# Hybrid block: the first down projection by seven products of quarter blocks per pair of outputs

## The reference

```python
def conv_ffn(h, w_up, conv_w, w_down):
    up = causal_dwconv(h @ w_up, conv_w)
    gate, val = jnp.split(up, [D_FF], axis=-1)
    return (jax.nn.silu(gate) * val) @ w_down
...
        h = rmsnorm(x, norm_ffn_g[l])
        x = x + conv_ffn(h, w_up[l], ffn_conv_w[l], w_down[l])
```

## Time and profile before

| | |
|---|---|
| runs | 1265.39 us median of 3 (1264.82 to 1266.54) |
| profiled execution | 1264.99 us, span 1263.3 us |
| PE, PEld busy | 1248.4 us (99%), 1003.6 us (79%) |
| DVE, ACT, POOL busy | 832.2 us (66%), 581.1 us (46%), 223.5 us (18%) |
| DMA | 130.01 MB, mean 103 GB/s |
| chain that ended last | PE 95%, of it line 842 82% |

### The profile page before, as it was taken

The page is one execution under the profiler, slowest core; times in us unless marked ns, Lnnn a source line. Parts: engine busy times, 40 slices in busy tenths (PEclk is TensorE's granted clock), DMA queues, the critical chain, the costliest instruction groups (busy, mean ns, idle before and its releaser), DMA issues.

```text
span 1263.3 us, 20146 instructions
## 1 busy us (share of the span) xinstructions
PE 1248.4 (99%) x6625; PEld 1003.6 (79%) x6625; DVE 832.2 (66%) x1709; ACT 581.1 (46%) x1053; POOL 223.5 (18%) x476
## 2 busy tenths in 40 slices
PE   8999999999999999999999999999999999999998
PEld 6777878878788788888888888888888776777776
DVE  6978777787777843444477773367764687794743
ACT  6655545445455432223344442244444465666632
POOL 2613304033040300001300000000004124440021
PEclk9999999999999999999999999999999999999999
DMA  6345263452634533333233323333224344333221
GB/s 191 76 118 142 73 152 91 117 132 78 156 89 119 131 102 85 99 100 100 84 102 99 100 75 100 113 95 100 81 84 109 102 117 118 84 87 97 81 71 67
DMA packets 283492, 130.01 MB, mean 103 GB/s; under 512 B 77296, under 2 KB 276271, under 8 KB 283445
## 3 DMA queue, kind: packets, MB, share of 16 engines
q1 hardware_dynamic: 283445, 129.42, 37.7%
HBM read 119.34 MB, written 10.06 MB: 102 GB/s over the span
## 4 chain that ended last, share of the span: by engine, by line
PE 95%; DVE 2%; ACT 1%; issue 1%; DMA 1%; SPq 0%; POOLq 0%; DVEq 0%; POOL 0%; ACTq 0%
PE gb L842 82%; PE gb L1290 2%; PE gd L1290 1%; PE gd L1240 1%; PE gd L1230 1%; PE gd L1218 1%; PE gd L935 1%; PE gd L943 1%; PE gd L1013 1%; PE gd L1024 1%; DMA raw<-in_w_in_dram 1%; DVE wlo L1843 0%; PE gd L1002 0%; ACT whi L1340 0%; PE gd L1001 0%
## 5 line engine op out<-in xcount | busy, mean ns | idle before, releaser
L842 PE MATMUL gb<-act_a,whi 128*128 128x512 f32 x2656 | 888.7, 398 | 0.3 <-DVE wlo L1843 0.2
L842 PEld LDWEIGHTS gb<-act_a,whi 128*128 128x128 f32 x2656 | 498.9, 188 | 111.9 <-issue 9.9
L842 PE MATMUL gb<-act_a,wlo 128*128 128x512 f32 x1408 | 548.9, 390 | 0.0
L1843 DVE TENSOR_TENSOR wlo<-raw,whi 128x1024 fp32r<-128x1024 f32 (+1 forms) x197 | 235.6, 1196 | 136.6 <-ACT whi L1340 134.7
L1340 ACT ACTIVATE whi<-raw 128x1024 fp32r<-128x1024 f32 (+1 forms) x210 | 215.7, 1027 | 217.4 <-PE gb L842 191.4
L842 PEld LDWEIGHTS gb<-act_a,wlo 128*128 128x128 f32 x1408 | 265.1, 188 | 48.4 <-issue 0.5
L842 PE MATMUL gb<-act_b,whi 128*128 128x512 f32 x432 | 152.9, 393 | 0.9 <-DVE wlo L1843 0.9
L842 PEld LDWEIGHTS gb<-act_b,whi 128*128 128x128 f32 x432 | 81.1, 188 | 18.8 <-DVE wlo L1843 1.4
L2745 POOL TENSOR_TENSOR zs<-zs,ca 128x512 f32<-128x512 f32 x3 | 4.2, 1397 | 321.3 <-ACT ca L1343 321.3
L842 PE MATMUL gb<-act_b,wlo 128*128 128x512 f32 x128 | 49.9, 390 | 0.0
L2700 POOL TENSOR_TENSOR Ue<-Ue,elt 128x60 f32<-128x60 f32 (+14 forms) x120 | 45.0, 375 | 9.4
(11 more groups left out here) (494 smaller groups left out, 1497.2 us busy)
## 6 DMA issues: line engine op xcount, KB each, us to landing
raw<-in_w_in_dram SPq DMA_DIRECT2D x102, 512.0 KB, 3.7
raw<-in_w_up_dram SPq DMA_DIRECT2D x44, 512.0 KB, 3.7
raw<-in_w_down_dram SPq DMA_DIRECT2D x16, 384.0 KB, 3.1
raw<-in_w_down_dram SPq DMA_DIRECT2D x16, 320.0 KB, 3.0
raw<-in_w_a_out_dram SPq DMA_DIRECT2D x8, 512.0 KB, 4.0
raw<-in_w_b_out_dram SPq DMA_DIRECT2D x8, 512.0 KB, 3.6
raw<-in_w_o_dram SPq DMA_DIRECT2D x8, 512.0 KB, 3.5
raw<-in_w_out_dram SPq DMA_DIRECT2D x8, 512.0 KB, 3.6
```

The costliest lines, as they stand in the source:

```text
L842: ins = pe.matmul(gb[:, b, :], l, r, start=(first and m == 0), stop=(last and m == len(todo) - 1))
L1843: dve.tensor_tensor(wlo[:, i % 2, 0:k * P], raw[:, i % 4, 0:k * P], whi[:, i % 2, 0:k * P].bitcast(F32), ALU.subtract).then_inc(split_read ...
```

## The change

For f = 0 alone, the two outputs of a pair, the even and odd inner blocks, and the two halves of the tokens form a product of 2 by 2 by 2 blocks. The change makes it with seven block products in place of eight, at the price of sums of weights (`weight_sum`, 128x768 each, four per pair), sums of activations (`token_sum`, 256 columns each, four per turn), and sums of results, of which some are made in PSUM by letting P6, P7 and P3 add into banks of P1 and P5. Each block product is a unit of 18 TensorE products of 256 columns in place of 512.

- TensorE (`seven`): 4 pairs of 7 units of 18 products, 504 products of 256 columns.
- SP: four loads per pair into the four `raw` slots. From the second pair on, they wait until the sums of the pair before are made (`weights_added`). Before, each load waited for one split.
- ScalarE (`down_high`, `token_high`): 28 high parts of 768 columns in place of 16, and high parts of the token sums.
- VectorE: 28 low parts (`down_low`), 28 additions to `xT` (`down_out`; six of 256 columns per pair and one of 512), 14 of the 16 weight sums (`add_weights`, 128x768), and in the last turn three low parts of token sums (`token_low`).
- GpSimd: four token sums per up turn, their low parts for all but the last turn, and the first pair's first two weight sums.
- The f = 0 up turns are written out on ScalarE and VectorE where they were loops. High and low parts of even blocks are made for 256 tokens in place of 512.
- Semaphores get second uses and new names (`xT_ready` is `copied`, `hn_ready` is `scaled_or_added`, `zeros_ready` is `pool_tiles`).

```diff
+SEVEN = 7
+FIRST_PAIR = ("P1", "P5", "P2", "P4", "P6", "P3", "P7")
+OTHER_PAIR = ("P1", "P2", "P4", "P5", "P6", "P3", "P7")
+WEIGHTS_OF = {"P1": 0, "P2": 1, "P4": 3}
+SUM_OF = {"P5": 0, "P6": 1, "P3": 2, "P7": 3}
+SUM_AT = (1024, 1792, 2560, 0)
+BLOCKS = FF_CUT[0] // 2
+HALF = T // 2
...
+        def token_half(name, i, low):
+
+            first, second = slice(0, HALF), slice(HALF, T)
+            even, odd = (slot((FF_LO if low else FF_HI) + 2 * i + q) for q in range(2))
+            both, last = spare[3 * i + low], spare[3 * i + 2]
+            return {"P1": even[:, first], "P5": even[:, second], "P2": odd[:, first], "P3": odd[:, second],
+                    "P6": both[:, first], "P7": both[:, second], "P4": last[:, second if low else first]}[name]
+
...
+        def weight_sum(m):
+
+            return sums[:, SUM_AT[m]:SUM_AT[m] + BLOCKS * P]
...
-        N_UP[1] = N_DN[0] + 2 * KD
+        N_UP[1] = N_DN[0] + SEVEN * KD // 2
...
+        def weight_sums_done(p, m):
+
+            return 4 * p + ((1, 2, 3, 4) if p == 0 else (1, 3, 4, 2))[m]
...
+                if f == 0:
+                    even_odd = w_dn_v[:, 0:FF_CUT[0], :].rearrange("p (k s) n -> p k s n", s=2)
+                    for p in range(KD // 2):
+                        for m in (0, 2, 3, 1) if p else range(4):
+                            q, s = DOWN[m]
+                            if p == 0:
+                                sp.wait_ge(split_ready, N_DN[0] + m - 3)
+                            else:
+                                sp.wait_ge(weights_added, 4 * p - (1 if p > 1 and m != 1 else 0))
+                                used = [w for w, k in WEIGHTS_OF.items() if k == m]
+                                if used:
+                                    sp.wait_ge(split_ready, N_DN[0] + SEVEN * (p - 1) + pair_order(p - 1).index(used[0]) + 1)
+                            dst = raw[:, raw_at(p, m), 0:kh * P].rearrange("p (k n) -> p k n", k=kh)
+                            at = (2 * p + q) * P
+                            sp.dma_start(dst, even_odd[:, :, s, at:at + P]).then_inc(raw_landed[raw_at(p, m)], 16)
+                    sp.wait_ge(weights_added, 2 * KD)
+                    continue
+                for m, (q, s) in enumerate(DOWN_CROSSED):
...
+            def seven(p):
+
+                order = pair_order(p)
+                banks = ({"P1": gd[:, 0, :], "P2": gd[:, 1, :], "P4": gd[:, 2, :], "P5": gd[:, 3, :]} if p % 2 == 0 else
+                         {"P1": gb[:, 3, :], "P2": gb[:, 0, :], "P4": gb[:, 1, :], "P5": gb[:, 2, :]})
+                into = {"P6": "P1", "P7": "P1", "P3": "P5"}
+                read_first = {"P6": "P1", "P7": "P6", "P3": "P5"}
+                for at, name in enumerate(order):
+                    n = N_DN[0] + SEVEN * p + at
+                    pe.wait_ge(hi_ready, n + 1)
+                    if name in read_first:
+                        pe.wait_ge(out_read, R_DN[0] + SEVEN * p + order.index(read_first[name]) + 1)
+                    bank = banks[into.get(name, name)][:, 0:HALF]
+                    for j in range(BLOCKS):
+                        last = p == 0 and j == BLOCKS - 1
+                        if last and name in ("P1", "P2"):
+                            pe.wait_ge(up_hi, 2 * j + (1 if name == "P1" else 2))
+                        elif last and name in ("P5", "P6", "P4"):
+                            pe.wait_ge(copied, KD + 3 * j + 1 + ("P5", "P6", "P4").index(name))
+                        hi = whi[:, n % 2, j * P:j * P + P]
+                        pe.matmul(bank, hi, token_half(name, j, 0), start=(j == 0 and name not in into), stop=False,
+                                  skip_group_check=True)
+                        if last:
+                            continue
+                        if p == 0 and name in ("P1", "P2"):
+                            pe.wait_ge(up_lo, 2 * j + (1 if name == "P1" else 2))
+                        elif p == 0 and name == "P5":
+                            pe.wait_ge(pool_tiles, 1 + 3 * j + 1)
+                        elif p == 0 and name in ("P6", "P4"):
+                            pe.wait_ge(pool_tiles, 1 + 3 * j + (2 if name == "P6" else 3))
+                        pe.matmul(bank, hi, token_half(name, j, 1), start=False, stop=False, skip_group_check=True)
+                    pe.wait_ge(split_ready, n + 1)
+                    for j in range(BLOCKS):
+                        ins = pe.matmul(bank, wlo[:, n % 2, j * P:j * P + P], token_half(name, j, 0), start=False,
+                                        stop=(p > 0 and j == BLOCKS - 1), skip_group_check=True)
+                    if p == 0:
+                        j = BLOCKS - 1
+                        if name in ("P1", "P2"):
+                            pe.wait_ge(up_lo, 2 * j + (1 if name == "P1" else 2))
+                        elif name in ("P5", "P6", "P4"):
+                            pe.wait_ge(pool_tiles, 2 + 3 * j + ("P5", "P6", "P4").index(name))
+                        ins = pe.matmul(bank, whi[:, n % 2, j * P:j * P + P], token_half(name, j, 1), start=False, stop=True,
+                                        skip_group_check=True)
+                    ins.then_inc(unit_done, 1)
...
+            def down_high(n):
+
+                p, name = down_set(n)
+                if name in WEIGHTS_OF:
+                    m = WEIGHTS_OF[name]
+                    sc.wait_ge(raw_landed[raw_at(p, m)], raw_count(p, m))
+                    src = raw[:, raw_at(p, m), 0:BLOCKS * P]
+                else:
+                    m = SUM_OF[name]
+                    sc.wait_ge(weights_added, weight_sums_done(p, m))
+                    src = weight_sum(m)
+                sc.wait_ge(unit_done, n - 1)
+                sc.activation(whi[:, n % 2, 0:BLOCKS * P], src, ACT.Copy).then_inc(hi_ready, 1)
...
+            def down_low(n):
+
+                p, name = down_set(n)
+                src = raw[:, raw_at(p, WEIGHTS_OF[name]), 0:BLOCKS * P] if name in WEIGHTS_OF else weight_sum(SUM_OF[name])
+                dve.wait_ge(hi_ready, n + 1)
+                dve.tensor_tensor(wlo[:, n % 2, 0:BLOCKS * P], src, whi[:, n % 2, 0:BLOCKS * P].bitcast(F32),
+                                  ALU.subtract).then_inc(split_ready, 1)
...
+            def add_weights(m, p):
+
+                w = lambda k: raw[:, raw_at(p, k), 0:BLOCKS * P]
+                for k in ((2, 3), (0,), (1,), ())[m]:
+                    dve.wait_ge(raw_landed[raw_at(p, k)], raw_count(p, k))
+                if p:
+                    name = [s for s, k in SUM_OF.items() if k == m][0]
+                    dve.wait_ge(split_ready, N_DN[0] + SEVEN * (p - 1) + pair_order(p - 1).index(name) + 1)
+                elif m == 2:
+                    dve.wait_ge(out_read, R_DN[0])
+                elif m == 3:
+                    dve.wait_ge(pool_tiles, 1 + 3 * BLOCKS)
+                if m in (1, 2):
+                    dve.wait_ge(weights_added, weight_sums_done(p, m - 1))
+                a, b, op = ((w(2), w(3), ALU.add), (weight_sum(0), w(0), ALU.subtract), (w(1), weight_sum(1), ALU.subtract),
+                            (w(0), w(2), ALU.subtract))[m]
+                dve.tensor_tensor(weight_sum(m), a, b, op).then_inc(weights_added, 1)
+
...
+            def down_sums(n):
+
+                p, at = divmod(n - N_DN[0], SEVEN)
+                for m in ({2: (2, 3)} if p == 0 else {0: (3, 1), 1: (2,)}).get(at, ()):
+                    add_weights(m, p)
+                if at == SEVEN - 1 and p < KD // 2 - 1:
+                    add_weights(0, p + 1)
...
+            down_next(N_DN[0] + 3)
+            token_low("P6")
+            token_low("P4")
+            down_out(N_DN[0])
+            down_out(N_DN[0] + 1)
+            for n in range(N_DN[0] + 2, N_UP[1]):
+                down_out(n)
+                down_next(n + 2)
+                down_sums(n)
...
+            def token_sum(m, i):
+
+                g, t = gated(i), token_sums(i)
+                first, second = slice(0, HALF), slice(HALF, T)
+                dst, a, b = ((t[:, 0:HALF], g[:, second], g[:, first]), (t[:, T:T + HALF], vc[:, second], g[:, second]),
+                             (t[:, HALF:T], vc[:, second], t[:, 0:HALF]), (t[:, HALF + T:2 * T], vc[:, first], t[:, HALF:T]))[m]
+                pool.wait_ge(up_ready, 2 * i + (2 if m else 1))
+                if m >= 2:
+                    pool.wait_ge(scaled_or_added, KD + 4 * i + m)
+                pool.tensor_tensor(dst, a, b, ALU.subtract).then_inc(scaled_or_added, 1)
...
+            for i in range(BLOCKS):
+                if i:
+                    token_low("P6", i - 1)
+                    token_low("P4", i - 1)
+                token_sum(0, i)
+                if i < BLOCKS - 1:
+                    token_low("P5", i)
+                else:
+                    add_weights(0)
+                    add_weights(1)
+                for m in range(1, 4):
+                    token_sum(m, i)
```

(64 more changed lines are left out.)

151 lines of the change are left out of this document (131 added, 20 removed).

## The result

The changed kernel takes **1269.0 us** (median of 9 runs, 1268.0 to 1269.8) beside 1265.4 for the kernel before (9 runs): a ratio of 1.0028, 95% interval 1.0020 to 1.0037, so 3.6 us slower, where 2.7 less were forecast. The profiled execution took 1268.99 us, 4.0 more than that of before.

What follows compares the result with a forecast made beforehand. TensorE was taken to bound the kernel (busy 99%): 58.0 us of products plus waits of 0.5, 1.0, 2.0, 0.6 and 0.6 make a stage of 62.7 in place of 65.3 us, so 1262.7 us, range 1260 to 1267.

Steps and rivals of the forecast that it cites:

- TensorE's products: First down projection: 504 products of 256 columns at 115 ns take 58.0 us, a gain of 7.3 us before waits.
- the prediction's own upper case: First down projection with products at 120 ns and waits of 3.7 us: stage 64.2 us.
- What costs nothing: Up turns: added ScalarE work, GpSimd's 5.6 us of sums per turn and written-out loops cost no time.
- GpSimd and VectorE block each other: Rival, last up turn: token parts come 2 to 3 us late, stage 65.2, kernel 1265.3 us; chance 0.05.
- the rule: Skill's rule, doubted by the prediction: two-SBUF-input VectorE instructions contend with GpSimd ones reading SBUF; the loser waits a whole instruction.
- The five waits: TensorE waits in the first and second pair and behind the stage: 0.5, 1.0, 2.0, 0.6 and 0.6 us.
- wait 3: Before P2 of the second pair: its weights, loaded last behind the first pair's sums, come late; 2.0 us.
- wait 4: Before P5 of the second pair: its low part comes late in VectorE's list; 0.6 us.
- waits 1 to 3: Before P6 and P3 of the first pair and P2 of the second: 0.5, 1.0 and 2.0 us.
- VectorE the bound: Rival, the stage's pairs: extra cost per VectorE instruction makes its list the limit, kernel 1270 us; chance 0.17.
- Writing out, up turns, ScalarE: Up turns: written-out loops are free, and ScalarE gains some 1.5 us per turn but stays under 21.8 us.
- Products that don't shrink: Rival, first down projection: 256 column products take 215 ns, stage 108 us, kernel 1308 us; chance 0.04.

Runs made afterwards that it cites:

- e4: The kernel before, with each first down projection product of 512 columns issued as two of 256; 1269.16 us.
- e7: The kernel before, with each first down projection product issued as two, of 384 and 128 columns; 1282.24 us.
- e1: The changed kernel, with the first pair's first two weight sums made by VectorE in place of GpSimd; 1268.15 us.
- e3: The changed kernel with the edits of both e1 and e2; 1264.74 us.
- e5: The kernel of e3, with the last turn's three token sums moved from GpSimd to VectorE and VectorE's list reordered as TensorE needs the parts; 1262.89 us.
- e6: The kernel of e3, with three GpSimd subtractions that nobody waits for where its two weight sums stood; 1266.29 us.
- e2: The changed kernel, with the second and fourth pair's weights loaded into idle space so the second pair's loads don't wait for the first pair's sums; 1266.11 us.

## Why the prediction was wrong

The forecast was a stage of 62.7 us and 1262.7; it came out as 68.45 and 1269.0, beyond the range's end at 1267. The 5.75 us that separate the two stages have two main parts.

**TensorE's products** (58.0 us forecast, 60.5 measured; 2.5 us). The mechanism was right and the size off. The 512 column row of this form allows 113.4 ns or, if the extra falls on each product alike, 120.0; the prediction took 115, "near the proportional end", because the fp32 rows of 512 and 128 columns are nearly in proportion. That step failed: fp32 products are another form, and e4 shows 120 for this one. By e7 a product of 128 columns costs about as much here as in fp32, so the two forms do not scale alike. With 120 and its waits of 3.7 us, the prediction's own upper case (64.2) would have stood as the forecast: 1.1 us below before, no change that the runs can tell. (The sum for 109 ns is 54.9 + 6.5 = 61.4 us, not 61.6; nothing hangs on it.)

**"What costs nothing"** (3.2 us). GpSimd's work was costed at nothing, and the weight sums "ready before 0". They were ready (751.81, against the stage's start at 751.86), and their values delayed nobody. But while they ran, VectorE lost 1.0 us on a low part and 1.5 on two convolution steps, and from 758.9 to 762.6 another 1.6 us beside the token sums. ScalarE's SiLU and its high part for P5 stand behind that convolution. VectorE's chain, forecast to end at 7.65 us after the stage's start, ended at 11.1 (its last low part of a token sum, 256 wide, ended at 762.98). The waits for P5, P2 and P4 came of it, 3.17 us, of which the forecast had none. The weight sums made those for P5 and P2 (1.94 us): with these sums on VectorE, 0.36 is left (e1, e3). The token sums made that for P4 (1.23 us), which stays in e1 and e3 and falls to 0.57 in e5; there GpSimd was late itself, with 256 wide sums of 1.0 to 1.4 us where 0.7 was estimated. The prediction had named P4's wait as what comes if GpSimd is late in the last turn, and gave it no time.

The rival "GpSimd and VectorE block each other" named this mechanism, with a chance of 0.05, and let it delay token parts only; its price was 2.5 us above the forecast stage.
```profile
1039.00 0.42 DVE L2482 MAX8 small<-selb 128x8 f32<-128x256 f32 x1
1039.53 0.41 DVE L2483 MATCH_REPLACE8 selb<-small,selb 128x256 f32<-128x256 f32 x1
```

Other rows of the kernel before did speak for the rule. GpSimd's sums of line 2728 took 1.86 us, all six of them beside a VectorE step with two SBUF inputs (line 2343), where operations of the same size took 1.27 to 1.30 us with VectorE idle (line 2773). Two of each:

```profile
L2728 POOL TENSOR_TENSOR zs<-zs,ca 128x512 f32<-128x512 f32 x2 | 3.7, 1856 | 130.7 <-ACT ca L1343 130.7
```
```profile
L2773 POOL TENSOR_TENSOR vc<-gate,vc x2: 1268/1282/1297, 1156.6 to 1207.8; 128x512 f32<-128x512 f32 x2
```

After the change, e6 agrees with the rule (0.77 to 1.49 us per convolution step), and so does line 2612, which has one input in PSUM and is not held. That the loser waits for a whole instruction, which the section says outright only of VectorE's two-port modes, is partly borne out: e6's low part lost 0.25 us, the steps 0.7 each, with GpSimd's instructions at 1.46.

**The five waits** were right in place, and their sum is 4.65 us against 4.7. That is in part luck: wait 3 is 0.57 longer than forecast and wait 4 0.35 shorter, and waits 1 to 3 kept their sizes as VectorE's list and TensorE ran late by about as much. P6's low part was made at t = 13.4 (from the stage's start) in place of 9.9, and TensorE wanted it at 13.1 in place of 9.55. The sums were made at t = 15.1 in place of 11.6, the last load landed at 23.5 in place of 19.0, and TensorE was ready for it at 22.0 in place of 18.0. For waits 3 and 4 e2 shows the cause, loads behind sums.

**VectorE the bound** didn't happen: third and fourth pairs run at TensorE's pace without a wait, with VectorE busy 13.2 of 15.8 us. **Writing out, up turns, ScalarE**: nothing lost, as said; the turn stays at 21.76 us with GpSimd's 7.7 us in it, where 5.6 were forecast, since VectorE holds GpSimd there too (low parts of 256 columns take 1.79 us in some places and 0.74 in others). **Products that don't shrink**: no, at 256 columns.

The chances: 0.16 for slower was too little. A forecast at the edge of what the runs can tell, on a middle value between 109 and 120 ns that no row of this form supported, should not have had 0.51 for faster.

## What to carry to other kernels

Work moved to an idle GpSimd can cost VectorE time wherever VectorE runs instructions with two SBUF inputs: compare durations of single instructions, not busy shares, and look for a stretch where VectorE works from PSUM or idles, or where the critical engine has slack. Price a smaller product from the same form's own row, with its fixed part kept whole, and don't carry that below the columns that were measured: 256 columns cost 120 ns, 128 about 113. Seven products in place of eight were worth 4.8 us here (65.3 less 60.5), so little that one chain of loads behind sums ate 3 of them. Before counting such a gain, lay out who must be early at the border of the stage; with spare buffers, these sums on VectorE and its list reordered, the same algorithm did win, by 0.19% (e5).

## What the runs showed of the hardware

A wait can cost more than its length. In e1, TensorE stood still for 2.5 us before P2 of the second pair. Busy time by stretch in e1 (columns as in the earlier trace rows, the granted clock third from the end):

```profile
770.00:772.00 2.00, 1.60 (x14) 1.40 (x12) 0.72 (x2) 0.00 (x0) 0.00 (x0) 1.00 0.66 193
772.00:774.00 2.00, 0.05 (x1) 0.05 (x1) 0.07 (x1) 0.94 (x2) 0.00 (x0) 0.89 0.02 7
774.00:775.00 1.00, 1.00 (x5) 1.00 (x6) 1.00 (x2) 0.64 (x1) 0.00 (x0) 0.50 0.00 0
...
776.00:777.00 1.00, 1.00 (x7) 1.00 (x6) 1.00 (x3) 0.00 (x0) 0.00 (x0) 0.51 0.00 0
777.00:778.00 1.00, 1.00 (x10) 1.00 (x10) 1.00 (x2) 0.21 (x1) 0.00 (x0) 1.00 0.00 0
```

Behind it the clock is 0.50, which is 1.2 GHz, for 3 us; the products are 213 ns apart, and 1.4 us are lost on top of the wait. The profiled execution of the change waited 2.5 us in the same place with the clock at 1.00:

```profile
774.00:776.00 2.00, 0.00 (x0) 0.00 (x0) 0.00 (x0) 0.60 (x1) 0.00 (x0) 1.00 0.04 11
```

So the same wait may or may not be followed by it. The mean clock of whole executions agrees: it is 0.997 or 0.998 in 8 of 11 of e1 and in 3 of 9 of the change (these three took 1269.4 to 1269.8 us), and 0.999 or more in all 43 of e2, e3, e5 and e6, which have no such wait.

Most waits inside TensorE's stream also cost some 0.1 us beyond themselves: the distance after one is 222 ns in place of 120 (24.44 to 24.66 us after the stage's start, before P2 of the second pair), as the prediction had added.
